# A two-layer diffusion step with a recurrence, attention and experts: dot products moved into the recurrence heads, keys turned between projections, and an output scaling moved behind products

## The reference, cut to what matters

```python
o_rec, s_f, s_b = hgrn2_branch(hq, hff, hfb, hi, hg, ...)
q = rms_norm(aq.reshape(B, L, ATTN_HEADS, HEAD_DIM), q_norm_g)
k = rms_norm(ak.reshape(B, L, KV_HEADS, HEAD_DIM), k_norm_g)
...
o_att = attend(axial_rope(q, rows),
               jnp.concatenate([axial_rope(k, rows), ctx_k], axis=1),
               jnp.concatenate([v, ctx_v], axis=1))
...
a = jax.nn.gelu(jnp.einsum('td,thkd->thk', xb, u_tab[eb]), approximate=False)
return jnp.einsum('thk,thkd->td', gb * a, v_tab[eb])
```

## Time and profile before

| | |
|---|---|
| median of three runs | 5514.78 us (5514.37 to 5520.26) |
| the profiled execution's own time | 5514.83 us |
| its span in the trace | 5512.9 us |
| PE busy | 4464.5 us, 81% of the span |
| DVE busy | 3395.8 us, 62% |
| POOL busy | 2126.0 us, 39% |
| ACT busy | 1508.3 us, 27% |
| mean granted TensorE clock | 0.943 of full speed |

### The profile page before, as it was taken

The page is one execution under the profiler, slowest core; times in us unless marked ns, Lnnn a source line. Parts: engine busy times, 40 slices in busy tenths (PEclk is TensorE's granted clock), DMA queues, the critical chain, the costliest instruction groups (busy, mean ns, idle before and its releaser), DMA issues. The chain is left out here.

```text
span 5512.9 us, 63669 instructions
## 1 busy us (share of the span) xinstructions
PE 4464.5 (81%) x18920; PEld 2395.5 (43%) x18920; DVE 3395.8 (62%) x6888; ACT 1508.3 (27%) x3912; POOL 2126.0 (39%) x1814
## 2 busy tenths in 40 slices
PE   7889997889595777777787899978895957777776
PEld 6556653446352323222265566535462523232222
DVE  2357776427778766754533677764187887677545
ACT  2112223520011333333321123135100113334333
POOL 0002125613656454455500021255036564445554
PEclk8999998999797999999999999989997989999999
DMA  7655447976989999999957454578679899999998
GB/s 271 254 199 182 141 163 263 335 255 251 372 319 341 420 420 417 416 421 418 404 215 271 173 180 143 195 263 325 238 274 364 327 342 420 420 413 416 420 419 345
DMA packets 299169, 1712.36 MB, mean 311 GB/s; under 512 B 34384, under 2 KB 44240, under 8 KB 178768
## 3 DMA queue, kind: packets, MB, share of 16 engines
q0 software_dynamic: 258048, 1342.29, 62.3%
q1 hardware_dynamic: 23712, 338.18, 16.2%
q10 hardware_dynamic: 17072, 27.83, 1.6%
HBM read 1694.53 MB, written 5.24 MB: 308 GB/s over the span
## 5 line engine op out<-in xcount | busy, mean ns | idle before, releaser
L430 POOL DMA_INDIRECT arena<-in_peer_uv,eidx x856 | 949.4, 1109 | 1200.6 <-POOLq L429 1004.5
L970 PE MATMUL banks<-arena 128*128 128x512 f32 x896 | 496.1, 636 | 238.2 <-PEq L1594 236.9
L2315 DVE SCALAR_TENSOR_TENSOR arena<-arena 128x1024 f32<-128x1024 f32 x384 | 470.7, 1226 | 350.4 <-DMA arena<-in_peer_uv,eidx 340.3
L482 POOL DMA_INDIRECT arena<-in_peer_uv,eidx x384 | 494.3, 1287 | 481.2 <-POOLq L481 458.4
L943 PE MATMUL banks<-ring,arena 128*128 128x512 f32 x864 | 384.8, 600 | 114.1 <-PEq L925 114.1
L972 PE MATMUL banks<-arena 128*128 128x512 f32 x896 | 472.1, 609 | 0.0
L534 ACT ACTIVATE arena<-arena 128x1 f32<-128x1 f32 (+1 forms) x770 | 156.2, 203 | 1039.4 <-ACTq L533 1039.2
L545 ACT ACTIVATE arena<-ident,arena 128x128 f32<-128x128 f32 x832 | 333.6, 401 | 301.0 <-ACTq L544 298.1
L970 PEld LDWEIGHTS banks<-arena 128*128 128x128 f32 x896 | 153.3, 195 | 549.0 <-issue 548.1
L1990 DVE SCALAR_TENSOR_TENSOR arena<-arena 128x1024 f32<-128x1024 f32 x256 | 308.4, 1224 | 99.6 <-DMA arena<-in_peer_uv,eidx 80.4
L2325 DVE SCALAR_TENSOR_TENSOR arena<-arena 128x1024 f32<-128x1024 f32 x256 | 307.0, 1225 | 98.8 <-DMA arena<-in_peer_uv,eidx 91.9
(11 more groups left out here) (319 smaller groups left out, 7573.5 us busy)
## 6 DMA issues: line engine op xcount, KB each, us to landing
ring<-in_wblk SPq DMA_DIRECT2D x160, 2048.0 KB, 8.5
arena<-in_peer_uv,eidx POOLq DMA_INDIRECT x1240, 7.2
arena<-arena ACTq DMA_DIRECT2D x64, 128.0 KB, 6.2
arena<-in_lnrows ACTq DMA_DIRECT2D x6, 1024.0 KB, 9.0
ring<-in_peer_uv,eidx POOLq DMA_INDIRECT x360, 6.6
arena<-in_sk ACTq DMA_DIRECT2D x4, 1024.0 KB, 7.6
hT<-in_peer_uv,eidx POOLq DMA_INDIRECT x192, 14.1
x<-in_x_sample ACTq DMA_DIRECT2D x1, 2048.0 KB, 28.5
```

The source lines that it names most:

```text
L430: nc.gpsimd.indirect_dma_start(row_buf[j], None, ins["peer_uv"], bass.IndirectOffsetOnAxis(ap=eidx[:, n, c:c + 1].bitcast(U32), axis=0)).t ...
L482: nc.gpsimd.indirect_dma_start(gslot[j], None, ins["peer_uv"].rearrange("(e h) d -> e (h d)", h=2), bass.IndirectOffsetOnAxis(ap=eidx[:, n ...
L970: nc.tensor.matmul(banks[:, b, :], diag[n], row[:, 0:CB], start=start, stop=stop, skip_group_check=True).then_inc(diag_used, 1)
L2315: V.scalar_tensor_tensor(u, u, 1.0, h2[:, t - 2, :], ALU.mult, ALU.mult, accum_out=av[:, r:r + 1])
```

## The change

The change does four things. It moves products: nine instead of seven in each recurrence head, eight and eight instead of 22 and four around the key normalisation, six behind the query normalisation, and 18 instead of 30 in the steps, which now take them in steps 0 to 11 (two in each of the first six, one in each of the next six) and no longer in steps 12 and 13. It moves `finish(n - 1)` in a step from ahead of the products to behind them and behind the normalisation part. It turns the keys on PE after projection g = 8 and the first queries after g = 10, instead of both after g = 11, and ACT's square roots and copies move with them. It moves the regrouping of gates on ACT (sixteen small copies) into the first four heads, and the last two replications of token vectors to earlier places.

```diff
-HEAD_ROWS = 7
-KEY_ROWS = 22
-QUERY_ROWS = 4
-STEP_ROWS = [3, 3] + [2] * 12
+HEAD_ROWS = 9
+KEY_ROWS = 8
+QUERY_ROWS = 8
+SCORE_ROWS = 6
+STEP_ROWS = [2] * 6 + [1] * 6
...
-        dots_end = GATE_ROWS + HEADS * HEAD_ROWS + KEY_ROWS + QUERY_ROWS
+        dots_end = GATE_ROWS + HEADS * HEAD_ROWS + KEY_ROWS + QUERY_ROWS + SCORE_ROWS
...
                     if h % 2 == 0:
                         replicate(2 + h // 2)
+                    if h == HEADS - 1:
+                        replicate(6)
+                    if h < REPS:
+                        regroup_gates(h)
...
+                    if g == LT:
+                        square_root(LT * KV)
                     if g == LT + 1:
-                        square_root(LT * KV)
-                        replicate(6)
-                    if g == 2 * LT + 1:
+                        replicate(7)
+                    if g == 2 * LT:
                         square_root(LT * 8)
-                        replicate(7)
-                for kp in range(2):
-                    arrived(2 * kp)
-                    nc.scalar.copy(KT[:, kp, :], pair(2 * kp, KEYS)).then_inc(bank_free[2 * kp], 1)
-                    act.drain().then_inc(kt_ready, 1)
+                        for kp in range(2):
+                            arrived(2 * kp)
+                            nc.scalar.copy(KT[:, kp, :], pair(2 * kp, KEYS)).then_inc(bank_free[2 * kp], 1)
+                            act.drain().then_inc(kt_ready, 1)
+                    if g == 2 * LT + 2:
+                        arrived(4)
+                        nc.scalar.copy(qTs[0], banks[:, 4, :]).then_inc(bank_free[4], 1)
+                        act.drain().then_inc(query_ready, 1)
...
+                    if g == 2 * LT:
+                        turn_keys()
+                    if g == 2 * LT + 2:
+                        turn_first_queries()
...
                     dve.drain().then_inc(sc_ready, 1)
-                    ctx_rows(HEAD_ROWS - 4)
+                    ctx_rows(HEAD_ROWS - 5)
...
                     if more:
                         decays(1 - b)
-                    ctx_rows(1)
+                    ctx_rows(2)
...
                 dve.drain().then_inc(qn_ready, 1)
+                ctx_rows(SCORE_ROWS)
...
                     invert(n)
-                    if n:
-                        finish(n - 1)
...
                     spread_ahead(n)
+                    if n < len(STEP_ROWS):
+                        ctx_rows(STEP_ROWS[n])
                     batch, part = (0, n) if n < 7 else (1, n - 9)
                     if 0 <= part < 7:
                         head_norm(512 + 256 * batch, 4, P, part, *narrow)
                         if part == 6:
                             dve.drain().then_inc(qn_ready, 1)
-                    if n < len(STEP_ROWS):
-                        ctx_rows(STEP_ROWS[n])
+                    if n:
+                        finish(n - 1)
```

53 lines of the change are left out of this document (27 added, 26 removed).

## The result

The changed kernel takes 5441.12 us (median of 4 runs, 5433.32 to 5446.53) against 5517.52 us (4 runs) of the kernel before on the same chip. The ratio is 0.9858, 95% interval 0.9838 to 0.9878: faster by 1.4%. The forecast was 5450, range 5428 to 5474. The profiled execution took 5435.86 us with a span of 5434.0 (before: 5512.9), so 78.9 us are to be found in the trace.

The account below looks back on a forecast made before the run. Taken as bound: PE in the heads, DVE ahead of the first scores, gathered rows in steps 0 to 16. Terms -5.8, -9.6, -7.1, -3.4, -5.2 make -31.1, second layer -33.4: -64.5 from 5514.83 gives 5450, range 5428 to 5474.

Parts of the forecast that it names:

- Two more products in each head: Recurrence heads: added DVE products fall into waiting, except in the last head; price +0.9 us a layer.
- Keys turned between projections: Between heads and steps: first scores start at 870.5 instead of 876.25, PE's chain late next; -5.8 us a layer.
- Steps 0 and 1: First two attention steps: without a third product, no wait for a slot freed in the same step; -9.6 us.
- Steps 2 to 5: Attention steps still with six gathered rows each: 4 x 8.6 = 34.4 us, gain 0.
- `finish` behind the products gains nothing here, since what ends a step is the gather.: Attention steps 2 to 5: moving `finish` was put at gain 0, the gather running beside its wait for `sums_ready`.
- Steps 6 to 11: five rows of 1.44 us each: Attention steps with one product: 7.2 us each plus 1 for ACT's tables, 44.2 us from 51.3; gain -7.1.
- Steps 12 to 16: Attention steps with four rows: 12 and 13 take 14.3 us (-3.4), 14 to 16 take 19.5 (-5.2).
- The gathers are not the limit: Rival, attention steps: with fewer waits POOL stays ahead and PE sets the steps; 5433 us, chance 0.17.
- The late slots stay the limit: Rival, attention steps: a gather's way and back sets 8.6 us, even with one product; 5464 us, chance 0.08.
- Slower through late `finish`: Rival, steps with products: late `out_free` holds PE's product with the values; up to 5556 us, chance 0.04.
- one of the signs named for being wrong: Wrong if heads take 44 us or more, PE idles ahead of L1450's successor, or one-row steps take 8.6.
- The heads did hide the products: Answers a rival, recurrence heads: products not hidden, `o1` late, PE waits; 5484 us, chance 0.09.

Follow-up runs that it names:

- half sum rows: Changed kernel gathering only the first half of each sums' row (2 KB in place of 4 KB per entry); ratio 0.9851 to the kernel before.
- three late slots: Changed kernel with a third slot for the products' rows in the steps; ratio 0.9864 to the kernel before.
- ten in heads: Changed kernel with ten products a head, 8 ahead of the first scores, one in each of the first eight steps; 5423.96 us, ratio 0.9835.
- nine in heads: Kernel before with nine products a head and 6 in place of 22 after the keys; ratio 0.9998 on the slow chip, 0.9987 on a usual one.

## Why the prediction was right, and where it was not

The time, 5441, lies in the range and 9 us under the forecast of 5450. The parts, in the prediction's order:

- **Two more products in each head.** Forecast +0.9 us a layer, all in the last head. From the output products of head 6 to those of head 7 it was 42.64 us in place of 41.56 in the first layer (+1.1), and 42.49 in place of 41.53 in the second (+1.0). From head 0 to head 7 it was +1.4 and +0.5. Right.
- **Keys turned between projections.** Forecast first scores 6.7 us earlier after the start of the projections (5.8 and the 0.9 of the heads). Measured -6.7 and -6.9. Right in its sum and in what is late next (PE's chain, 1.61 us ahead of the scores). The heading names the keys' turning, but the experiments give most of it to the fewer and moved products, 5.6 of 7.0, and 1.4 to the turning.
- **Steps 0 and 1.** Forecast 17.0, measured 17.3. Right: with a third product gone, so is the wait for a slot freed in the same step.
- **Steps 2 to 5.** Forecast 34.4, measured 33.3, and 34.0 to 34.8 in the other traces. Right, at 8.3 to 8.7 us a step.
- **"`finish` behind the products gains nothing here, since what ends a step is the gather."** This is the step that failed. Put back, `finish` costs 5.6 us a layer. The clearest part is step 11, 10.5 and 12.1 us against 7.8 in both layers of every kernel with 18 products and `finish` last on these chips. Steps 2 to 5 are some 3 us longer, too (37.2 and 36.9 against 33.3 to 34.8), but "half sum rows" and "three late slots" reached 36.3 and 36.8 there with `finish` last, so that part is within what repeats. In the kernel before the move is worth 1.5 us a layer, within what repeats, but not for the reason given: there PE waits 26.0 us for the late `finish`.
- **Steps 6 to 11: five rows of 1.44 us each.** Forecast 44.2, measured 40.5 and 41.2. Mis-sized: steps 8 to 10 are PE's 6.2 us, so a row came in 1.25 us or less. The 1.44 us were read as a rate of the DMA engines from their share of 0.98. Halving the bytes of four rows in six left the steps as they were at a share of 0.71, so that was not a limit. The trace of the kernel before had a sign of it outside the stretch: in a later stage, from 1800 to 1900 us, the same DMA engines move 420 GB/s at a share of 1.01, in place of 368 at 0.98.

```profile
1800.00:1900.00 100.00, 75.89 (x156) 29.42 (x155) 78.22 (x225) 34.53 (x116) 42.89 (x40) 0.95 1.01 420
```

What is full in the steps of two products is GpSimd's issuing: 0.94 + 0.30 us, plus what VectorE's products add. Fewer products in a step make that smaller, too.
- **Where the 9 us come from.** The forecast's steps 0 to 16 add up to 129.4 us; measured were 124.5 in the first layer and 125.5 in the second: 4.9 and 3.9 less, of which 3.7 and 3.0 are steps 6 to 11. The 11 us of `finish` are no further term beside this. Without them steps 6 to 11 took 42.4 and 45.7, in the mean the 44.1 of the forecast, though steps 8 to 10 were at 6.2 to 6.4 there as well and step 11 made up for it. So it was partly luck that the forecast of the time came so near: a rate that was too slow stood for a cost of the old order that was put at nothing.
- **Steps 12 to 16.** Forecast 14.3 and 19.5; the starts of DVE's minima give 13.95 and 19.45. Right.
- **The rivals.** "The gathers are not the limit" (5433) had the truth for steps 8 to 10 but not for steps 2 to 5, which stayed at 8.3 to 8.7 us each; the result stands between it and the forecast. "The late slots stay the limit" fell with the third slot. "Slower through late `finish`" is a real mechanism, and one of the signs named for being wrong, PE idle ahead of the products with the values, did come: 4.0 and 3.2 us a layer here, 26.0 in the kernel before with `finish` last. It stayed far under the 2.7 us a step that would have decided. The heads did hide the products.

What stays open: how the 5.6 us of `finish` divide between DVE's own lateness and GpSimd's stops (both are seen, neither was removed alone), what GpSimd's issuing would give back if its issues were not lengthened, and what makes one chip's rows slow.

## What to carry to other kernels

A saturated-looking share of the DMA engines doesn't say that bytes are the limit: halve the bytes, and look at whether the issuing engine has any idle time but its fixed gap. In an in-order engine, a wait for another engine belongs behind the work that is ready, but this only pays when that work isn't itself late, for what the moved instruction releases comes late with it (PE's 26.0 us): a cause that is worth nothing in the kernel before can be worth something in the kernel after, so it has to be judged with the other parts of the change in place. Work that fits beside a bound stage (here ten products in a head) is to be moved there until the stage begins to grow, and then weighed: 2.6 us a layer paid against 10.9 gained.

## What the runs showed of the hardware that was not expected

**GpSimd's issues and VectorE's operations with two SBUF inputs.** In steps 0 to 16 of the first layer of six traces (both kernels, the changed kernel again, half rows, three slots, ten in heads), 180 issues of a gather began while VectorE ran an operation with two inputs in SBUF; 111 of them took over 1.1 us, up to 2.00. Of the 331 others, among them 151 beside a reduction with one input, none did; their mean was 0.94. The lengths follow one sum: all 130 issues that began with 0.15 to 1.25 us of such an operation left took what was left of it plus 0.81 us, within 0.01. Seven that began in its last 0.06 us took 1.98 to 2.00. Of the 69 that stayed under 1.1 us, 67 began in its last 0.29 us, where this sum gives little more than 0.94; the other two began within 0.03 us of its start. The Trainium skill, "SBUF — State Buffer", in its part on the two separate sides, says that the two engines share a port pair that is locked for a whole instruction, with a VectorE operation that has two SBUF inputs as one of the cases; the trace agrees, in which operations do it (111 against 0) and in that the issue waits until the operation's end. The page's section on who interferes with whom limits that case to GpSimd instructions that read SBUF. No run here tells a read from a write of GpSimd.

**A chip with slow gathers.** On one chip the same gathers came at 293 GB/s with a DMA share of 0.86 where they made 326 at 0.92 elsewhere, and steps 2 to 13 took 10.3 us in the mean ("nine in heads") in place of 8.6; the kernel before was 1.3 to 1.4% slower there (5590.94 against 5521.48 and 5514.53). The order of `finish` was worth 13 us a layer there and 5.6 elsewhere.

**The clock.** The first scores took 2.08 us at a granted clock of 0.65 after a wait of 5.87 us. With waits of 1.61, or 0.71 and 2.10 us, they took 1.13, and the granted clock of the stretch from 859.41 to 868.04 of the changed kernel was 1.00: full speed, 2.4 GHz. The prediction had left this "some 1 us less" in its range; it came out so.
